# Every second pair of plain one-hot rows of the gate matrix built by GpSimd instead of VectorE

## What is computed

```python
def peer_chunk(h, w_q, sub_keys, u_tab, v_tab):
    C = h.shape[0]
    q = (h @ w_q).reshape(C, PEER_HEADS, 2, D_KEY // 2)
    s = jnp.einsum('cphd,phkd->cphk', q, sub_keys).astype(jnp.float32)
    s1, i1 = lax.top_k(s[:, :, 0], PEER_TOPK)
    s2, i2 = lax.top_k(s[:, :, 1], PEER_TOPK)
    ...
    e = jnp.take_along_axis(cidx, top_i, axis=-1)
    g = jax.nn.softmax(top_s, axis=-1)
    a = jax.nn.gelu(jnp.einsum('cpkd,cd->cpk', u_tab[e], h)).astype(jnp.float32)
    return jnp.einsum('cpk,cpkd->cd', (g * a).astype(v_tab.dtype), v_tab[e])
```

## Time and profile before

| what | value |
|---|---|
| median of 3 runs | 1236.09 us (1236.05 to 1238.46) |
| the profiled execution's own time | 1229.46 us |
| its span, first to last instruction | 1227.8 us |
| mean granted TensorE clock in it | 0.948 |
| busy in the span | PE 97%, PEld 91%, DVE 70%, ACT 48%, POOL 10% |
| gate stage, first to last pair on TensorE | about 684 to 831 us |

### The profile page before, as it was taken

How to read it: one execution, slowest core, us unless ns; L and a number is a source line. 1 busy time by engine, 2 the same in 40 slices (tenths; PEclk the granted TensorE clock), 3 DMA queues, 4 the chain that set the end, 5 groups by cost and what they waited for, 6 DMA issues and landing times.

```text
span 1227.8 us, 27046 instructions
## 1 busy us (share of the span) xinstructions
PE 1191.3 (97%) x8948; PEld 1115.1 (91%) x8948; DVE 862.4 (70%) x1964; ACT 589.4 (48%) x1105; POOL 127.5 (10%) x136
## 2 busy tenths in 40 slices
PE   7999999999899999999999999998999999999996
PEld 7974777767799999999999999998999999999995
DVE  4320224324678898988875899996888888888885
ACT  5432753224344544444446455554555555555553
POOL 0424000003000010005520000001011010010000
PEclk9999875569999999999999999998999999999998
DMA  6758211002423577669997444446888787887861
GB/s 249 287 166 304 106 45 69 1 1 69 147 94 121 187 265 267 232 227 375 413 390 252 149 142 149 134 148 220 274 273 272 274 277 269 274 274 269 275 232 39
DMA packets 96681, 252.07 MB, mean 205 GB/s; under 512 B 11136, under 2 KB 44976, under 8 KB 96096
## 3 DMA queue, kind: packets, MB, share of 16 engines
q1 hardware_dynamic: 82160, 195.81, 46.4%
q0 software_dynamic: 14480, 55.75, 13.0%
HBM read 231.46 MB, written 22.12 MB: 207 GB/s over the span
## 4 chain that ended last, share of the span: by engine, by line
PE 90%; DMA 5%; DVE 2%; ACT 2%; issue 1%; SPq 0%; ACTq 0%; DVEq 0%
PE ps L489 22%; PE ps L491 22%; PE ps L490 22%; DMA activations<-u_out 5%; PE ps L879 5%; PE ps L585 3%; PE ps L732 2%; PE ps L612 1%; PE ps L718 1%; PE ps L825 1%; PE ps L704 1%; PE ps L694 1%; PE ps L814 1%; PE ps L810 1%; PE ps L716 1%
## 5 line engine op out<-in xcount | busy, mean ns | idle before, releaser
L1235 DVE TENSOR_TENSOR w_lo<-ring,w_hi 128x512 fp32r<-128x512 f32 (+1 forms) x458 | 388.6, 851 | 141.1 <-ACT w_hi L932 125.8
L932 ACT CAST w_hi<-ring 128x512 fp32r<-128x512 f32 (+1 forms) x460 | 346.0, 752 | 107.9 <-PE ps L491 104.0
L489 PE MATMUL ps<-h_hi,w_hi 128*128 128x256 f32 (+1 forms) x1152 | 339.8, 295 | 5.3 <-DVE h_lo L1496 4.8
L491 PE MATMUL ps<-h_hi,w_lo 128*128 128x256 f32 (+1 forms) x1152 | 326.8, 284 | 0.0
L490 PE MATMUL ps<-h_lo,w_hi 128*128 128x256 f32 (+1 forms) x1152 | 324.3, 282 | 0.0
L489 PE MATMUL ps<-y_hi,w_hi 128*128 128x256 f32 x1024 | 291.2, 284 | 4.2 <-DVE y_lo L1662 4.2
L490 PE MATMUL ps<-y_lo,w_hi 128*128 128x256 f32 x1024 | 291.0, 284 | 0.0
L491 PE MATMUL ps<-y_hi,w_lo 128*128 128x256 f32 x1024 | 291.0, 284 | 0.0
L489 PEld LDWEIGHTS ps<-h_hi,w_hi 128*128 128x128 f32 x1152 | 218.2, 189 | 10.1 <-DVE h_lo L1496 5.3
L490 PEld LDWEIGHTS ps<-h_lo,w_hi 128*128 128x128 f32 x1152 | 218.2, 189 | 0.0
L491 PEld LDWEIGHTS ps<-h_hi,w_lo 128*128 128x128 f32 x1152 | 217.4, 189 | 0.0
(11 more groups left out here) (339 smaller groups left out, 1472.0 us busy)
## 6 DMA issues: line engine op xcount, KB each, us to landing
ring<-in_uT_dram SPq DMA_DIRECT2D x128, 512.0 KB
ring<-in_v_dram SPq DMA_DIRECT2D x128, 512.0 KB
activations<-u_out SPq DMA_DIRECT2D x128, 128.0 KB
a_in<-activations SPq DMA_DIRECT2D x128, 128.0 KB, 4.1
ring<-in_w_in_dram SPq DMA_DIRECT2D x22, 512.0 KB
kvs<-in_cache_sb_dram POOLq DMA_DIRECT2D x16, 512.0 KB, 6.9
ring<-in_w_q_dram SPq DMA_DIRECT2D x16, 512.0 KB
ring<-in_w_out_dram SPq DMA_DIRECT2D x8, 512.0 KB
```

What stands on the lines that cost most here:

```text
L489: mm(out, hi, hi_, start=start, stop=False)
L491: return mm(out, lo, hi_, start=False, stop=stop)
L932: nc.scalar.copy(w_hi[slot][:, x], ring[:, ring_slot, x]).then_inc(part_hi, 2 if half is None else 1)
L1235: V.tensor_tensor(w_lo[slot][:, x], ring[:, ring_slot, x], w_hi[slot][:, x].bitcast(F32), ALU.subtract).then_inc(part_lo[ring_slot], 2 if ...
```

## The change

GpSimd builds the plain rows of the odd pairs, `one_b[1]`, with two `tensor_scalar` instructions per pair (one per token), and counts them on a new semaphore `two_ready`. VectorE still builds all gated rows, and the plain rows of the even pairs. TensorE waits for both engines before an odd pair. In GpSimd's program the new block stands between the gathers of `urow` and those of `vrow`. The loop variable `k` of the gathers is renamed `j`, since `k` is needed as the function that names constants.

```diff
             pool.wait_ge(ix_ready, 1)
...
-                nc.gpsimd.indirect_dma_start(urow[:, k % 4, :], None, u_rows, at_slot(k)).then_inc(ug_in[k % 4], 16)
...
+                nc.gpsimd.indirect_dma_start(urow[:, j % 4, :], None, u_rows, at_slot(j)).then_inc(ug_in[j % 4], 16)
+            pool.wait_ge(rt_slot, 3)
+            for m in range(DT // 4):
+                pool.wait_ge(g_mm, 2 * m + 2)
+                for t in range(2):
+                    at_t = slice(4 * m + 2 + t, 4 * m + 3 + t)
+                    ins = nc.gpsimd.tensor_scalar(one_b[1][:, t, :], k("iota"), slotT[:, 1, at_t], None, ALU.is_equal)
+                ins.then_inc(two_ready, 1)
             v_rows = v.rearrange("j p d -> (j p) d")
...
                         pe.wait_ge(one_ready, 16 * i + (4 * r + q + 1))
+                        if q % 2 == 1:
+                            pe.wait_ge(two_ready, 8 * i + (2 * r + q // 2 + 1))
...
-                            V.tensor_scalar(one_a[:, q % 2, t, :], k("iota"), slotT[:, 0, at_t], slotT[:, 2, at_t],
-                                            ALU.is_equal, ALU.mult)
-                        V.tensor_tensor(one_b[q % 2][:, :, :], k("iota").unsqueeze(1).to_broadcast([128, 2, 128]),
-                                        slotT[:, 1, bass.ds(32 * i + t0, 2)].unsqueeze(2).to_broadcast([128, 2, 128]),
-                                        ALU.is_equal).then_inc(one_ready, 1)
+                            ins = V.tensor_scalar(one_a[:, q % 2, t, :], k("iota"), slotT[:, 0, at_t],
+                                                  slotT[:, 2, at_t], ALU.is_equal, ALU.mult)
+                        if q % 2 == 0:
+                            ins = V.tensor_tensor(
+                                one_b[0][:, :, :], k("iota").unsqueeze(1).to_broadcast([128, 2, 128]),
+                                slotT[:, 1, bass.ds(32 * i + t0, 2)].unsqueeze(2).to_broadcast([128, 2, 128]), ALU.is_equal)
+                        ins.then_inc(one_ready, 1)
```

More of the change, by code:

```diff
@@ L322, in trunk @@
         rt_exp_in, rt_exp, rt_pick, rt_t, rt_slot = map(sem, ("rt_exp_in", "rt_exp", "rt_pick", "rt_t", "rt_slot"))
-        u_act, one_ready, g_mm, g_sb = map(sem, ("u_act", "one_ready", "g_mm", "g_sb"))
+        u_act, one_ready, two_ready, g_mm, g_sb = map(sem, ("u_act", "one_ready", "two_ready", "g_mm", "g_sb"))
         spill = [sem(f"spill{r}") for r in range(2)]
@@ L462, in _ @@
             pool.dma_start(keys[:, :, :], keysT).then_inc(keys_in, 16)
-            at_slot = lambda k: bass.IndirectOffsetOnAxis(ap=expert[:, k:k + 1], axis=0)
+            at_slot = lambda j: bass.IndirectOffsetOnAxis(ap=expert[:, j:j + 1], axis=0)
             pool.wait_ge(ix_ready, 1)
-            for k in range(SLOTS):
-                if k >= 4:
-                    pool.wait_ge(u_dot, k - 3)
-                nc.gpsimd.indirect_dma_start(urow[:, k % 4, :], None, u_rows, at_slot(k)).then_inc(ug_in[k % 4], 16)
+            for j in range(SLOTS):
+                if j >= 4:
+                    pool.wait_ge(u_dot, j - 3)
+                nc.gpsimd.indirect_dma_start(urow[:, j % 4, :], None, u_rows, at_slot(j)).then_inc(ug_in[j % 4], 16)
[6 more added lines that the diff above has]
+                ins.then_inc(two_ready, 1)
             v_rows = v.rearrange("j p d -> (j p) d")
[L471 to L474, removed]
+            for j in range(SLOTS):
+                if j >= 2:
+                    pool.wait_ge(v_acc, j - 1)
+                nc.gpsimd.indirect_dma_start(vrow[:, j % 2, :], None, v_rows, at_slot(j)).then_inc(vg_in[j % 2], 16)
         @block.tensor
```

## The result

The changed kernel took 1250.43 us (median of 4 runs, 1247.12 to 1252.35) against 1236.07 us for the kernel before (4 runs): a ratio of 1.0124, interval 1.0073 to 1.0175. It is slower by 1.2%, which is clear of the noise. The time lies inside the range and far from the 1236.9 us that was named. Timed again in E9, with more runs of both, the ratio is 1.0179 (1.0138 to 1.0219), 22.4 us between the medians. Ratios leave out the executions that took over 1.5% longer than the fastest of their kernel, so one can differ a little from the ratio of the two medians beside it. The profiled execution took 1252.35 us, 22.9 us more than the one of before.

What follows compares the result with a forecast made beforehand. The prediction took TensorE to bound the gate stage. Its sum was 1229.46 + 0 + 0 + 0.8 = 1230.3 us for the profiled execution; the same 0.8 on the median of the runs gave 1236.9 us, range 1235.0 to 1256.

Steps and rivals of the forecast that it cites:

- What bounds the kernel: Gate stage: TensorE sets the pace at 1.15 us a pair; VectorE's loop happens to fill it exactly.
- Rival C: Gate stage: VectorE sets the pace, so the change is faster, by 21 us at most; chance 0.05.
- What the change removes: Gate stage: 64 VectorE instructions, 21.4 us in all; gain 0, but 0.335 us of slack per two pairs.
- What it adds on GpSimd: Gate stage: 128 tensor_scalar of 128 columns, taken at 0.3 us each, with 0.2 to 0.4 as bounds.
- Is it in time: Odd pairs' rows on GpSimd: about 1.2 us needed of 1.58 us available, fitting by 0.4.
- What the two engines cost each other: Gate stage lock: a GpSimd instruction of length H pushes VectorE back about H - 0.2; at 0.3, slack covers it.
- The gathers: First two vrow gathers, issued later, run where the first a_in loads are issued: 0.8 us, bounds 0 and 2.0.
- A: Gate stage: GpSimd's lock makes VectorE late; slower by 4, 12.5 (1249.4 us) or 30 us; chance 0.28.
- B: Gate stage: GpSimd's rows come late for TensorE; 8 us at 0.4 us each, 20 to 33 more at 0.6; chance 0.12.

Runs made afterwards that it cites:

- E9: The changed kernel, unedited, timed again beside the kernel before: 1251.38 us against 1228.99, ratio 1.0179.
- E1: Kernel before without plain rows for odd pairs on any engine, TensorE multiplying those pairs with the identity: ratio 1.0002.
- E5: Changed kernel with a second buffer for odd pairs' plain rows, so GpSimd may be one odd pair ahead, and vrow gathers first: ratio 1.0005.
- E7: As E2, with GpSimd's first instruction of each pair cut from 128 to 32 columns: 1233.42 us in one run.
- E3: Changed kernel with VectorE's low half in the gate stage cut from 512 to 8 columns: ratio 1.0039.
- E10: Kernel before with only its first two vrow gathers moved late, GpSimd making no rows: ratio 1.002.
- E2: Changed kernel with TensorE neither waiting for nor reading GpSimd's plain rows, identity in their place for odd pairs: ratio 1.0016.

## Why the prediction was right in its range and wrong in its number

**What bounds the kernel** held. The reading of the first pairs was confirmed by E1: 1.15 us a pair is TensorE's own. Rival C was priced at up to 21 us and given 0.05; it measured 0.

**What the change removes** held: VectorE's slack is there, 14.1 us of waits in 56 rounds of E5, mostly 0.21 each. The 35 us of the changed kernel have the longer stage in them.

**What it adds on GpSimd** is the step that failed. I took 0.3 us an instruction with 0.2 to 0.4 as bounds; it is 0.58 from start to start, outside them. The memset that bounded it from below reads nothing, and I halved its time as if it had no fixed part. The line that bounded it from above has 1024 columns, among which a fixed 0.25 us, as E7 has it, can't be seen. I gave it a fixed part of 0.1 without a row for it.

**Is it in time** failed with it, and by a second term: "up to 0.26 for one VectorE instruction that may stand between them" was 0.55, since it was not an `one_a` that stood there but the low half. The forecast sum 1.2 became 1.90 against 1.58.

**What the two engines cost each other** had the lock right and its direction wrong. By my formula two instructions of 0.58 would have pushed VectorE back by 0.76 us. By the waits of E1 and E5 it lost nothing. In rows 7 GpSimd was running when VectorE came, so VectorE was held. Here the low half starts 0.04 us after GpSimd's second instruction, and it is GpSimd that is held (E3 shows it by taking the low half away). The Trainium skill's SBUF — State Buffer, section "Who interferes with whom", says that the order of issue decides who blocks, and that the loser blocks for the whole instruction. The trace agrees with the second part as far as GpSimd goes, which ended 0.39 us after the low half did; on the first, the start in the trace doesn't decide, since it was 0.04 us earlier for GpSimd. E7 brackets what does: for this instruction a low half that starts up to 0.23 us behind it holds it, and one that starts 0.36 us behind doesn't. That GpSimd takes its access only at its first read, after its fixed 0.25 us, would explain both; that reason itself isn't shown. The two-source GpSimd instruction of rows 7 held VectorE already at 0.18.

**The gathers** were priced at 0.8 with bounds 0 and 2.0. They cost 2.4 in the changed kernel and 4.6 alone (E10). The step "the first gather can use the idle DMA just before" has nothing in the runs for it.

**The rivals.** A, given 0.28 and a middle price of 1249.4 us, is near the measured 1250.43 by coincidence: E2 shows that its mechanism costs the stage at most 0.4 us. B is what happened, and its line "with 0.6 each the same comes out as 1.9 to 2.1, 20 to 33 us more" is met by 1.90 us and 21.8. I gave it 0.12, because I judged it at 0.3 to 0.4 us an instruction and treated 0.6 as an afterthought. The chance of slower, 0.44, was the sum of the right case and a wrong one. That the time lies in the range is luck too: the upper end of 1256 was set by A's price and by B at 8 us, and what B cost at 0.6 us was left above it. From the 1236.09 us on which the range was built, the 24.2 us of the trace lead to 1260.3, outside; the time came out lower because the runs of the kernel before had lain high (E9).

## What to carry to other kernels

When two engines both look full in a stage, look where one has a lead it can't lose, as in the first pairs: that tells which sets the pace, and work taken from the other buys slack alone. Before moving work to an engine that has never run the instruction, price the fixed part by itself (here 0.25 of 0.58 us), and add to the path from the releasing event to the consumer whatever the other engine may run in between; a second buffer, cheap here (E5), takes that path away. And a transfer that moves down a queue must be placed in time against the loads on the critical path, not only against its own consumer.

## What the runs showed of the hardware that I had not expected

- A GpSimd `tensor_scalar` of fp32 with a pointer: 0.58 us from start to start for 128 columns, 0.33 for 32, so 0.25 us fixed and 2.6 ns a column (E2, E7). An estimate worked out from the Trainium skill's GPSIMD Engine Reference, section 3.1, is 0.19 us plus dispatch for 128.
- VectorE's fp32 `tensor_scalar`, at 0.5 ns a column, was hardly held by a GpSimd instruction in the changed kernel: the two `one_a` at 741.76 beside it took 0.61 us together, against 0.60 alone, and GpSimd's took 0.60 with them and 0.60 without VectorE beside it (its second one at 674.77 us in the changed kernel, VectorE's line 1244 having ended at 674.30). In E7, at another offset, one `one_a` took 0.43 us and not 0.34. The Trainium skill's SBUF — State Buffer, section "Who interferes with whom", counts such an instruction among those that contend; the traces agree, but show 0.09 us at most, where the two-source low half cost GpSimd 0.55.
- Which of the two is held depends on the offset: GpSimd's 128-column instruction took 1.15 us with the low half 0.04 us behind it (changed kernel), 1.31 with 0.23 and 0.60 with 0.36 (both E7).
- Two gathers issued 2.1 and 0.9 us ahead of four loads of 128 KB delayed TensorE's start by about 4.6 us (E10: gap 8.9 us for 4.2 to 4.4), although VectorE needed the gathered rows much later.
- The granted clock in the first 345 us was 0.83 to 0.89 in the mean from run to run, and the gate stage began between 670.5 and 691.4 us accordingly. Why it differs was not studied.
